# Linear attention evicted by pairs of units, and the routing asks for the second block's weights

## The reference, cut to what matters

```python
def step(s, inp):
    qc, kc, vc, ac = inp
    b = jnp.cumsum(ac, axis=2)
    rel = jnp.where(causal[:, :, None], b[:, :, :, None, :] - b[:, :, None, :, :], -jnp.inf)
    a_intra = jnp.einsum('bhtsd,bhsd->bhts', qc[:, :, :, None, :] * jnp.exp(rel), kc)
    o = (jnp.einsum('bhts,bhsv->bhtv', a_intra, vc)
         + jnp.einsum('bhtd,bhdv->bhtv', qc * jnp.exp(b), s))
    ...
```

```python
pad_end = jnp.cumsum(padded)
blk_expert = jnp.minimum(jnp.searchsorted(pad_end, jnp.arange(n_blocks) * MOE_BLOCK, side='right'), N_EXPERTS - 1)

def expert_block(args):
    xb, e = args
    g, u = jnp.split(xb @ w_up[e], 2, axis=-1)
    return (jax.nn.silu(g) * u) @ w_down[e]
```

## Time and profile before

| | |
|---|---|
| time, median of 3 runs | 2990.88 us (2987.67 to 2993.07) |
| the profiled execution | 2991.17 us, of which span 2989.3 us |
| PE busy | 2831.2 us, 95% of the span |
| DVE busy | 1419.7 us, 47% |
| ACT busy | 808.2 us, 27% |
| POOL busy | 64.8 us, 2% |
| HBM traffic over the span | 140 GB/s |
| mean granted TensorE clock | 0.976 of full |

### The profile page before, as it was taken

The page is one execution under the profiler, slowest core; times in us unless marked ns, Lnnn a source line. Parts: engine busy times, 40 slices in busy tenths (PEclk is TensorE's granted clock), DMA queues, the critical chain, the costliest instruction groups (busy, mean ns, idle before and its releaser), DMA issues. The chain is left out here.

```text
span 2989.3 us, 44002 instructions
## 1 busy us (share of the span) xinstructions
PE 2831.2 (95%) x18377; PEld 1675.9 (56%) x18377; DVE 1419.7 (47%) x1968; ACT 808.2 (27%) x1503; POOL 64.8 (2%) x90
## 2 busy tenths in 40 slices
PE   8999999999999989999999998999989699999995
PEld 4434564444444434444454445656455699999994
DVE  6843676566666663444643007867664311111113
ACT  2111572111111114334200106756412211111111
POOL 0000000000000000000000000000000000000002
PEclk9999999999999999999999999999999899999997
DMA  3112751211111124333231000013200899999995
GB/s 136 53 49 36 213 206 39 82 43 43 43 42 43 43 104 187 137 137 121 63 68 63 29 0 11 1 35 90 90 6 10 321 400 402 399 402 402 402 356 179
DMA packets 118420, 409.91 MB, mean 137 GB/s; under 512 B 9536, under 2 KB 28480, under 8 KB 113568
## 3 DMA queue, kind: packets, MB, share of 16 engines
q1 hardware_dynamic: 98480, 374.35, 34.4%
q0 software_dynamic: 6000, 21.37, 2.2%
q10 hardware_dynamic: 13824, 12.59, 1.2%
HBM read 367.38 MB, written 51.38 MB: 140 GB/s over the span
## 5 line engine op out<-in xcount | busy, mean ns | idle before, releaser
L3182 PE MATMUL ex_up_ps<-big,ex_xT 128*32 128x384 f32 x3072 | 345.5, 490 | 16.1 <-issue 9.1
L3184 PE MATMUL ex_up_ps<-big,ex_xT 128*32 128x128 f32 x3072 | 349.7, 274 | 0.0
L3184 PEld LDWEIGHTS ex_up_ps<-big,ex_xT 128*32 128x32 f32 x3072 | 331.8, 110 | 0.6
L1927 PE MATMUL dn_acc<-big,V 128*128 128x512 f32 x704 | 304.9, 596 | 1.6 <-PEq L43 1.6
L1927 PEld LDWEIGHTS dn_acc<-big,V 128*128 128x128 f32 x704 | 134.4, 191 | 170.5 <-issue 170.5
L1542 PE MATMUL fm_ring<-h,V 128*128 128x512 f32 x504 | 219.7, 592 | 0.0
L937 PE MATMUL f_acc<-h,f_w 128*128 128x512 f32 x416 | 180.7, 593 | 0.0
L3184 PE MATMUL ex_y_ps<-ex_wd,ex_hT 128*32 128x128 f32 x1536 | 175.5, 275 | 0.0
L293 DVE TENSOR_SCALAR_CACHE_REDUCE h<-ad_s_ps 128x1280 f32<-128x1280 f32 x64 | 92.9, 1489 | 172.6 <-PE ad_s_ps L202 172.6
L3182 PE MATMUL ex_y_ps<-ex_wd,ex_hT 128*32 128x384 f32 x1536 | 173.4, 492 | 0.8 <-DVE ex_hT L3326 0.8
L3184 PEld LDWEIGHTS ex_y_ps<-ex_wd,ex_hT 128*32 128x32 f32 x1536 | 169.3, 111 | 0.6
(11 more groups left out here) (548 smaller groups left out, 4535.1 us busy)
## 6 DMA issues: line engine op xcount, KB each, us to landing
big<-in_w_eup SPq DMA_DIRECT2D x32, 4096.0 KB
ex_wd<-in_w_edown SPq DMA_DIRECT2D x32, 2048.0 KB, 22.8
fm_up<-in_w_up SPq DMA_DIRECT2D x22, 1028.0 KB, 4.9
y_dram<-in_cos SPq DMA_DIRECT2D x1, 21504.0 KB, 73.9
dn_tail<-in_w_mod SPq DMA_DIRECT2D x32, 512.0 KB, 6.9
V<-in_w_down SPq DMA_DIRECT2D x8, 1408.0 KB, 6.9
y_dram<-big ACTq DMA_DIRECT2D x32, 288.0 KB
dn_tail<-in_w_in SPq DMA_DIRECT2D x17, 512.0 KB, 3.6
```

What stands on the lines that cost most here:

```text
L1927: mm = nc.tensor.matmul(o[:, x * BANK:(x + 1) * BANK], wd[j % 2][:, k * P:(k + 1) * P], hidden[:, k, x * BANK:(x + 1) * BANK], start=(k == ...
L3182: nc.tensor.matmul(o[32 * g:32 * g + 32, 0:W], rows(g), w[:, 0:W], start=first, stop=last)
L3184: mm = nc.tensor.matmul(o[BR:P, g * P:(g + 1) * P], rows(g), w[:, W:BANK], start=first and g == 0, stop=last and g == GR - 1)
```

## The change

Three edits are made together.

- In `gla_and_out`, `keep` takes the units it is to keep, and both lists interleave keeping by pairs of units with the making of factors two levels ahead. S is scaled behind level 2 instead of before level 1.
- In `route`, the block table is made with the blocks on partitions (one comparison of 32 columns, a reduction, a minimum), turned into one row by a matmul (`block_ps`), and kept before `ids`. `slot` is written last. SP reads the expert of block 1 here, waits for `x_ready[0]` and asks for its up weights. The scratch `spare` gets a tile of its own, since half 1 of `wu` is now written inside this phase.
- In `experts`, SP's wait, its first read and that load are gone, and PE and ACT read the number of used blocks only before their loops.

```diff
@@ scalar, gla_and_out
                 power(1)
+                for n in by_act:
+                    keep(n, (0, 1))
+                    power(2 * n)
+                    keep(n, (2, 3))
+                    if n == by_act[0]:
+                        power(2 * n + 1)
                 act.wait_ge(u_used, 2 * C)
                 for y in range(4):
                     mine = S[:, :, :, 64 * y:64 * y + 64].rearrange("p d c v -> p (d c) v")
                     nc.scalar.activation(mine, mine, ACT.Copy, scale=cst["heads32"][:, y:y + 1]).then_inc(state_ready, 1)
-                for n in range(1, N + 1):
-                    if n < N:
-                        power(n + 1)
-                    if n in by_act:
-                        keep(n)
+                for n in range(5, N + 1):
+                    power(n)
@@ vector, gla_and_out
                 dve.wait_ge(masks_in, 16)
-                for n in range(2, N + 1):
-                    weigh(n)
-                    if n < N:
-
-                        dve.wait_ge(unit_ready, 4 * (n - 1))
-                        arguments(n + 1)
-                    keep(n - 1)
-                    add_part(5 + n)
-                keep(N)
+                arguments(3)
+                weigh(2)
+                for n in range(1, N + 1):
+                    keep(n, (0, 1))
+                    if n >= 2:
+                        if n + 2 <= N:
+                            dve.wait_ge(unit_ready, 4 * n)
+                            arguments(n + 2)
+                        add_part(5 + n)
+                    keep(n, (2, 3))
+                    if n + 2 <= N:
+                        weigh(n + 2)
                 add_part(6 + N)
@@ route
-        spare = big[:, 11:16, :].rearrange("p a n -> p (a n)")
+        spare = ph.sb("spare", [P, 3072])
...
                 load_up(sp, din, sp.value_load(r["first"][0:1, 0:1], min_val=0, max_val=E_ - 1), wu, 0, u_ready)
+                sp.wait_ge(block_kept, 1)
+                second = expert_of(sp, r, 1)
+                sp.wait_ge(x_ready[0], 16)
+                load_up(sp, din, second, wu, 1, u_ready)
...
                 mm.then_inc(listed_ready, 1)
+                pe.wait_ge(evicted, TT)
+                pe.wait_ge(block_made, 1)
+                nc.tensor.matmul(block_ps, bex[0:NB], cst["ident"][0:NB, 0:NB], start=True, stop=True).then_inc(block_turned, 1)
...
                 st.done(V_.tensor_copy(r["count"], cnt))
+                st.done(V_.tensor_scalar(begun, incl, cst["token"][:, 0:1], None, ALU.is_le))
+                st.done(V_.tensor_reduce(bex, begun, AX.X, ALU.add))
+                V_.tensor_scalar(bex, bex, float(E_ - 1), None, ALU.min).then_inc(block_made, 1)
                 dve.wait_ge(listed_ready, 1)
                 V_.tensor_copy(listed[:], listed_ps).then_inc(listed_kept, 1)
-                V_.tensor_copy(r["slot"], slotf)
+                dve.wait_ge(block_turned, 1)
+                V_.tensor_copy(r["block"][0:1, :], block_ps).then_inc(block_kept, 1)
                 dve.wait_ge(ids_ready, 1)
                 V_.tensor_copy(r["ids"][0:BR, 0:NB], ids_ps[0:BR]).then_inc(ids_kept, 1)
-                st.done(V_.tensor_tensor(cmp, incl.unsqueeze(1).broadcast_to([P, NB, E_]), wide(cst["block"], E_), ALU.is_le))
-                st.done(V_.tensor_reduce(bex, cmp, AX.X, ALU.add))
-                st.done(V_.tensor_scalar(bex, bex, float(E_ - 1), None, ALU.min))
-                V_.tensor_copy(r["block"], bex)
+                V_.tensor_copy(r["slot"], slotf)
@@ experts: sync, then tensor (scalar alike)
-                sp.wait_ge(x_ready[0], 16)
...
-                load_gate_up(0, 1)
                 load_down(0, 0, 0)
...
-                nb = used(pe)
...
                 product(0, 1, 1)
                 down(0, 0)
+                nb = used(pe)
                 with pe.Fori(1, NB // 2) as i:
```

More of the change, by code:

```diff
@@ L2565, in power, with keep @@
                     nc.scalar.activation(pairs[n % 3], pairs[n % 3], ACT.Exp, scale=1.0 / 16).then_inc(powers, 1)
-                def keep(n):
+                def keep(n, units):
                     m = GLA_HALVES[n - 1]
-                    for u in range(4):
+                    for u in units:
                         act.wait_ge(unit_ready, 4 * n + u + 1)
@@ L2703, in _ @@
                 add_part(2)
-                keep(0)
+                keep(0, range(4))
                 dve.wait_ge(powers, 1)
@@ L2780, in carve @@
             a, used[0] = used[0], used[0] + size
-            assert used[0] <= 5 * T
+            assert used[0] <= 3072
             x = spare[:, a:used[0]]
@@ L2787, in route @@
         g4, top = r["g4"], r["top"]
-        g4b, cmp = carve(TT, 4), carve(NB, E_)
+        g4b, begun = carve(TT, 4), carve(E_)
         c1, low, pg = (carve(TT) for _ in range(3))
         base, nblk, incl, onesr, total = (carve(E_) for _ in range(5))
-        bex, cnt, one_bex = carve(NB), carve(2), carve(1)
+        bex, cnt, one_bex = carve(1), carve(2), carve(1)
         slotf, blkf, lanef = carve(2, TT), carve(2, TT), carve(2, TT)
@@ L2813, in route @@
         listed_ready, listed_kept = ph.sem("listed_ready"), ph.sem("listed_kept")
+        block_made, block_turned, block_kept = ph.sem("block_made"), ph.sem("block_turned"), ph.sem("block_kept")
+        block_ps = acc[0:1, 0, 0:NB]
         with nc.Block() as block:
@@ L3258, in _ @@
             def _(act):
-                nb = used(act)
                 for s, n in ((stored[0], 16 * PARTS), (stored[1], 16 * PARTS), (xT_ready, 1), (silu_done, 1)):
@@ L3299, in _ @@
                 store_y(0, 0)
+                nb = used(act)
                 with act.Fori(1, NB // 2) as i:
```

## The result

The changed kernel takes 2962.95 us (median of 4 runs, 2960.96 to 2964.95); the kernel before, measured beside it, 2989.31 us (4 runs, 2987.67 to 2993.07). The forecast of 2970.5 started from a kernel before of 2990.88 us; of the 7.5 us between it and the measured time, 6.0 are a larger gain and 1.6 come from that start. The profiled execution took 2964.95 us (span 2963.1), 26.2 us less than that of before.

What follows compares the result with a forecast made beforehand. PE in levels 1 to 7 and the weights' stream in the experts were taken as bounds; 18.0 + 2.4 = 20.4 us off 2991.17 gives 2970.8, less 0.3 for the median: 2970.5 us, range 2966 to 2975.

Steps and rivals of the forecast that it cites:

- The walk through the attention's levels: Levels 1 to 7: new order traced with measured durations; pauses total 3.8 us, PE ends at 2215.3, 18.0 us saved.
- So the clock is not charged: Levels 1 to 7: no pause exceeds 0.75 us, so no lost clock is added to the 3.8 us of pauses.
- The rival of the falling clock: Levels: clock still falls at short pauses, five clusters at 2.3 us each, 11.5 us; 2982.0 us; chance 0.10.
- The price of the clock before: Levels of the kernel before: 9.7 of the 21.85 us missing against fourteen full turns were put down to lowered clock.
- Everything behind level 7 taken as unchanged: Rest of the attention and routing up to the first up load: 0 us of gain forecast.
- Their removal alone is worth nothing: Routing: the comparison and reduction on DVE lay beside POOL's drain of 6.07 us, so removing them gains nothing.
- SP last at the barrier: End of routing: the barrier waits for SP instead of POOL, 0.7 us later (bounds 0 and 0.8).
- Counts no longer read: Start of experts: PE and ACT no longer load the block count there, gaining 0.9 us (bounds 0.5 and 1.2).
- PE starts 0.2 us earlier: Start of experts: PE's start comes 0.2 us earlier, with the later barrier set against the block count no longer loaded.
- The early load: Experts: second up load starts 2.4 us earlier, the product that waited 2.65 us waits under 1; 2.4 us saved.
- the dry stream: Rival, experts: weights' stream has run dry when half 0 comes free, so early load buys nothing; 2972.7 us; chance 0.14.
- Costs a us at the worst: Experts: the weights' 2.4 us head start leaves the gather of the next tokens the same room, or costs at worst 1 us.

Runs made afterwards that it cites:

- fill: Kernel before, order kept, with two never-read matmuls ahead of the third unit of levels 1, 3, 4 and 5; 2985.15 us, ratio 0.9992 to the kernel before.
- tail_shift2: Kernel before with only the attention changed, plus two never-read matmuls ahead of the first matmul on S; 2968.81 us, ratio 0.9949 to the kernel before.
- tail_shift1: Kernel before with only the attention changed, plus one never-read matmul ahead of the first matmul on S; 2965.51 us, ratio 0.993 to the kernel before.
- keep_cmp: Changed kernel with the old comparison and reduction put back on DVE, result unread, scratch tile larger; 2961.81 us, ratio 0.9921 to the kernel before.
- late_load: Changed kernel with the second up load asked for in `experts`, as before; 2962.36 us, ratio 0.9927 to the kernel before.
- gather_both: Changed kernel with the second block's tokens also gathered in the routing, POOL's loop shifted by one gather; 2960.2 us, ratio 0.991 to the kernel before.
- s_first: Changed attention but S scaled before level 1 as before, routing as before the change; 2972.42 us, ratio 0.9958 to the kernel before.
- attn_only: Kernel before with only `gla_and_out` taken from the changed kernel; 2965.06 us, ratio 0.9927 to the kernel before.

## Why the prediction was off

The walk through the attention's levels held. Two steps failed, and both put at nothing what an edit does beside or behind itself. A third of the miss is variation that no edit made.

- **Levels, 18.0 forecast, 18.53 measured.** The walk held: no stop at level 1 (second pair 4.42 us behind the first), `power(4)` 14.8 us behind the first unit (14.7), 0.66 and 0.40 at level 3 (0.33 and 0.67), later ones only in levels 5 and 6, none in level 7: one of 0.36 us, and pairs of units longer by 0.20 to 0.57 us (0.39 to 0.75 forecast, in levels 5 to 7). All pauses together are 3.3 us, not 3.8: 65.34 less the 62.0 of fourteen turns.
- **"So the clock is not charged": right inside the levels.** Clock 1.00 in every window. The rival of the falling clock is out for these pauses. The Trainium skill (TensorE: Matmul & The Clock Gate, section "A second HAM failure mode: psum-queue depth-cycling") tells of a bf16 kernel in which short idling made the clock swing; this trace, in float32 and with pauses of up to 0.66 us, doesn't show it. The price of the clock before was read too high, 9.7 us where the windows give 7.9 (see fill); that changed nothing in the sum, which counts from 62.0 us of full turns.
- **Everything behind level 7 taken as unchanged: this step failed,** by 1.66 us in the tail and 0.63 in the routing. The prediction stopped reading the clock where the edit stopped. The tail ran below full clock before (12 matmuls in 7.99 us, where tail_shift2 shows 5.40), and tail_shift1 and 2 show that where and how long the clock is low moves with PE's work ahead of it. That it moved in the change's favour is luck: one extra matmul takes the tail back to 37.31.
- **"Their removal alone is worth nothing" (comparison and reduction): this step failed.** They lay beside POOL's drain, and the prediction took the drain for their cover. But the comparison made the gather's issue 1.52 us longer, and the drain waits for the gather. Expected "POOL's drain is as long as before"; it fell from 6.07 to 4.42. With the comparison back (keep_cmp) the second load comes 2.2 us earlier and the stretch is 2.7 shorter, about the 2.4 forecast; without it the load comes 4.0 to 4.2 earlier and the stretch is 3.4, 5.3 and 6.0 shorter in three profiles. So the hidden work was not free for the barrier; what it costs at the end is bounded by profiles and not seen in medians.
- **SP last at the barrier: right,** 1.0 us behind the drain's end (2323.42 to 2324.4), 0.7 forecast. Counts no longer read: forecast 0.9, and late_load shows PE 2.26 us earlier of which the shorter drain is 1.57, so 0.7. The forecast that PE starts 0.2 us earlier holds for neither kernel: 1.4 us with the shorter drain, 0.6 us later in keep_cmp.
- **The early load: right in kind.** The product that waited 2.65 us no longer does, and the dry stream is not seen. "Costs a us at the worst" for the second gather: 1.28 us, but from PE's earlier start, and not on the path (gather_both).
- **The sum.** Of the 5.8 us by which the profiled pair exceeds the forecast, 0.5 are levels, 2.3 tail and routing (all of it clock), 1.0 experts, and 2.0 the start of level 1 and the last phase, which vary without cause in the change. The medians show 26.4 in one batch and 24.4 in another, against 20.4. The range's lower end took in all pauses gone and 3.1 us in the experts, but neither the clock behind the edit nor anything over 3.1; these two were missing from the bounds.

**Open.** What decides where the clock falls: why it fell behind fill's stop of 1.71 us and not behind s_first's of 1.63 at the same place, and why tail_shift2's tail has no slow stretch. Why the experts' stretch of the same code took 604.9 and 603.0 us; with that spread, what the removed comparison is worth at the end (0.7 to 2.6 us by the profiles of the whole change) is bounded and not measured, and the medians of keep_cmp and of the changed kernel can't be told apart. Why tail_shift2, whose tail is the fastest, has a median 3.8 us above attn_only's.

## What to carry to other kernels

Work that lies beside a wait is free only if it can't lengthen what the wait is for: look at the duration of the instruction that is issued beside it, not only at the end of the wait. When a change moves PE's work by some us, read the granted clock and the durations of the stretch behind it as well, and allow for it: tail and routing together took 93.5 to 97.5 us here, the same instructions up to the routing's edit. A ring of two slots was kept in time once the keeping went by pairs: the longest piece of other work between two pairs of keeps (3.1 us), set against PE's turn of two units and half a part (4.43 us), predicted the levels' gain to 3%.

## What the runs showed of the hardware

- An indirect DMA's issue on POOL took 2.61 us beside a float32 comparison of 1792 columns with both inputs in SBUF, ending 0.96 us behind it, and 1.09 us without it.
- A stop of 1.71 us was followed by a lowered clock (0.69 over 11 us, fill); one of 1.63 us at the same place was not (s_first), nor one of 1.67 us two levels on (fill). The same stop of 1.97 us was followed by a clock of 0.83 over 10 us in three kernels and of 1.00 in tail_shift1. Shorter pauses, up to 1.25 us (s_first) and several in a row, left it at 1.00. The length of a stop alone doesn't decide.
- The same code of the tail took 33.93 us at full clock (one profile), and 35.62 or 37.3 us, each in several profiles, with a slow stretch in it.
- POOL's drain at the end of a phase lasts until its gather has landed (late_load: landing 4.2 us behind 2319.45, the drain's end at 2323.7): 4.42 to 4.75 us with the issue of 1.09 us, 6.0 to 6.4 with that of 2.61, 6.32 with two gathers, 8.54 beside a second 4 MB load.
